# Expert outputs scattered by token, padding rows skipped, and the pair sum of the tail on PE

## The reference

```python
# 32 experts in 4 groups; each token takes the best group and its two best experts there
gate = softmax(top_v) * pg[group]
for each (token, k) with expert e:
    h = silu(x[token] @ w_gate[e]) * (x[token] @ w_up[e])     # 1024 -> 512
    y[token] += gate[token, k] * (h @ w_down[e])              # 512 -> 1024
x = layer_norm(alpha * x + y, ln3_g, ln3_b)
```

## Time and profile before

| | us |
|---|---|
| median of 3 runs | 1987.08 (1986.65 to 1987.32) |
| the profiled execution | 1967.48 |
| its span | 1965.7 |

### The profile page before, as it was taken

How to read it: one execution, slowest core, us unless ns; L and a number is a source line. 1 busy time by engine, 2 the same in 40 slices (tenths; PEclk the granted TensorE clock), 3 DMA queues, 4 the chain that set the end, 5 groups by cost and what they waited for, 6 DMA issues and landing times. The chain is left out here.

```text
span 1965.7 us, 33639 instructions
## 1 busy us (share of the span) xinstructions
PE 1787.5 (91%) x14867; PEld 1130.0 (57%) x14867; DVE 756.5 (38%) x1109; ACT 309.8 (16%) x705; POOL 209.9 (11%) x196
## 2 busy tenths in 40 slices
PE   8999999999999779999998999958999999999960
PEld 4455567776664554444666666525666666666630
DVE  1111456535362653430011433363343333333339
ACT  1111223311010441111000211000110111111115
POOL 2100000000000420000000000013111111111016
PEclk9999999999999769999999999968999999999985
DMA  5251002001100202134211000246999999999966
GB/s 199 89 176 43 1 1 88 1 1 43 43 1 0 93 8 110 43 123 139 83 43 43 22 22 22 92 189 241 422 424 423 424 424 424 424 424 424 423 239 218
DMA packets 72865, 326.96 MB, mean 166 GB/s; under 512 B 13369, under 2 KB 27969, under 8 KB 59729
## 3 DMA queue, kind: packets, MB, share of 16 engines
q1 hardware_dynamic: 47840, 280.70, 35.5%
q10 hardware_dynamic: 17360, 22.03, 3.5%
q0 software_dynamic: 7584, 23.08, 3.2%
HBM read 288.05 MB, written 37.65 MB: 166 GB/s over the span
## 5 line engine op out<-in xcount | busy, mean ns | idle before, releaser
L785 PE MATMUL psum<-arena 128*32 128x256 f32 x6144 | 339.3, 380 | 31.9 <-issue 30.7
L418 PE MATMUL psum<-arena 128*128 128x352 f32 x1152 | 342.4, 460 | 0.0
L427 PE MATMUL psum<-arena 128*128 128x512 f32 (+1 forms) x720 | 319.2, 602 | 5.1 <-DMA arena<-in_w_in 3.9
L785 PEld LDWEIGHTS psum<-arena 128*32 128x32 f32 x6144 | 232.0, 110 | 138.1 <-issue 45.1
L418 PEld LDWEIGHTS psum<-arena 128*128 128x128 f32 x1152 | 219.4, 191 | 122.4 <-issue 1.4
L1371 DVE COPY arena<-psum 128x512 f32<-128x512 f32 (+7 forms) x135 | 90.9, 681 | 418.1 <-PE psum L427 221.9
L427 PEld LDWEIGHTS psum<-arena 128*128 128x128 f32 (+1 forms) x720 | 132.0, 186 | 177.1 <-issue 175.2
L794 PE MATMUL psum<-arena 128*32 128x256 f32 x3072 | 172.4, 379 | 0.5 <-DVE arena L1776 0.5
L794 PEld LDWEIGHTS psum<-arena 128*32 128x32 f32 x3072 | 117.2, 110 | 49.3 <-DVE arena L1776 1.0
L1082 ACT ACTIVATE arena<-psum 128x128 f32<-128x128 f32 (+5 forms) x181 | 86.5, 495 | 349.8 <-PE psum L411 276.2
L1969 POOL DMA_INDIRECT arena<-x_rows,consts x102 | 96.7, 948 | 410.0 <-DVE arena L1779 381.8
(11 more groups left out here) (254 smaller groups left out, 1434.7 us busy)
## 6 DMA issues: line engine op xcount, KB each, us to landing
arena<-in_moe_w_down SPq DMA_DIRECT2D x34, 2048.0 KB, 15.6
arena<-in_moe_w_gate SPq DMA_DIRECT2D x34, 2048.0 KB, 14.9
arena<-in_moe_w_up SPq DMA_DIRECT2D x34, 2048.0 KB, 22.0
arena<-in_w_in SPq DMA_DIRECT2D x7, 2048.0 KB, 9.1
y_blocks<-arena ACTq DMA_DIRECT2D x136, 96.0 KB, 26.8
y_blocks<-arena ACTq DMA_DIRECT2D x1, 8448.0 KB, 43.9
arena<-in_x_prompt SPq DMA_DIRECT2D x9, 512.0 KB, 3.3
arena<-in_w_out SPq DMA_DIRECT2D x2, 2048.0 KB, 10.7
```

The costliest lines, as they stand in the source:

```text
L418: last = mm(ps[0:m, c * BANK:c * BANK + THIRD], lhs(k), rhs[:, k, c * THIRD:(c + 1) * THIRD], start=(k == 0), stop=(k == KD - 1))
L427: last = mm(ps[0:n, c * 512:(c + 1) * 512], lhs(k), rhs(k, c), start=(k == 0), stop=(k == KD - 1))
L785: last = mm(out, xeT[:, b, a, k, :], gu[b][:, :, k, j * P:(j + 1) * P], start=(k == 0), stop=(k == KD - 1))
```

## The change

- The DRAM tensor `y_blocks` gives way to `y_pairs` with 2 x 1056 + 1 rows: row 1 + 2 t + k belongs to token t and its k-th expert. Row 0 isn't used. `x2_rows` gets a row more as well, and token t stands in row 1 + t.
- The table made by PE now carries 1 + 2 t + k instead of t, so a padding row gives 0. From it DVE makes `tok_idx` (with a rounding that undoes the doubling, six operations instead of one before the cast) and `y_idx` (two operations). Padding rows get an index of 65536 and more, beyond the bound, and indirect DMAs skip such rows (`bounds_check`, `oob_is_err=False`).
- The results of a block are stored by POOL with three indirect DMAs (`scatter`), in place of ACT's four plain ones. POOL's order in the expert stage is gather(e), scatter(e-4), gather(e+1), ...
- In the tail SP loads `y_pairs` with plain DMAs, one for each tile, the tile of 32 tokens first (`TAIL`). PE adds the two rows of each token by two products with the identity into PSUM for the eight whole tiles; DVE does the small one. DVE's and ACT's steps are the same, in the order of `TAIL`.
- `dest_i`, `zeros`, the fill of the overflow blocks and the waits on it are gone. POOL in place of ACT sets `fin_ready`.

```diff
-            link(STT(TB_, EE, float(C), RR, ALU.mult, ALU.add))
-            link(V.tensor_copy(dest_i.rearrange("p k t -> p (k t)"), TB_))
...
-            link(TS(tokq, both[:, 0], 4.0, quarter, ALU.mult, ALU.add))
+            link(TS(tokq, both[:, 0], 0.5, -0.75, ALU.mult, ALU.add))
+            link(TS(tokq, tokq, ROUND, -ROUND, ALU.add, ALU.add))
+            link(TS(padq, both[:, 0], 0.0, FAR, ALU.is_equal, ALU.mult))
+            link(TS(padq, padq, quarter, None, ALU.add))
+            link(STT(tokq, tokq, 4.0, padq, ALU.mult, ALU.add))
+            link(TS(tokq, tokq, 4.0, None, ALU.add))
             V.tensor_copy(tok_idx, tokq).then_inc(tables_ready, 1)
+            dve.wait_ge(tables_ready, 1)
+            link(STT(tokq, both[:, 0], 4.0, padq, ALU.mult, ALU.add))
+            V.tensor_copy(y_idx, tokq).then_inc(tables_ready, 1)
```

```diff
 # SP
+            sp.dma_start(x2_dram[0:1, :], x2[0:1, 0, :]).then_inc(x2_stored, 16)
 # ACT, y_rows
                 last.then_inc(y_ready, 1)
-                act.wait_ge(y_ready, e + 1)
-                store_y(y_dram[bass.ds(e * C, C), :], slot, y_out[slot])
 # ACT, spilled
-                store_y(y_dram[bass.ds(j * C + NE * C, C), :], b, o_out)
-                act.wait_ge(o_out, 64 * j + 64)
```

```diff
 # POOL
+            def scatter(e, slot, done):
+                for a in range(NS):
+                    pool.indirect_dma_start(out=y_quarters, in_=ye[slot][:, a, :], in_offset=None,
+                                            out_offset=bass.IndirectOffsetOnAxis(ap=y_idx[:, e, a:a + 1], axis=0),
+                                            bounds_check=4 * (2 * T + 1) - 1, oob_is_err=False)\
+                        .then_inc(done, 16)
+            for e in range(2, NE):
+                pool.wait_ge(xt_ready, e - 1)
                 gather(e, e % 2, xe_in[e % 2])
+                if e >= 4:
+                    scatter_expert(e - 4)
...
+                    pool.wait_ge(o_y, j + 1)
+                    scatter(NE + j, j % 2, o_out)
+                    pool.wait_ge(o_out, 48 * j + 48)
+                    link(Q.memset(quarter, 0.0))
+            for i in range(4):
+                pool.wait_ge(y_out[i], 48 * NE // 4)
+            Q.memset(quarter, 0.0).then_inc(fin_ready, 1)
```

```diff
 # SP
+            sp.wait_ge(fin_ready, 1)
+            for t in TAIL:
+                rows = y_dram[1 + 2 * t * P:1 + 2 * (t * P + rows_of(t)), :]
+                sp.dma_start(pairs[0:rows_of(t), t], rows.rearrange("(t k) n -> t k n", k=2)).then_inc(g_in[t], 16)
 # PE
+            for u in range(1, NT):
+                t = TAIL[u]
+                pe.wait_ge(g_in[t], 16)
+                if u >= 5:
+                    pe.wait_ge(sum_ready, u - 3)
+                for c in range(2):
+                    for k in range(2):
+                        last = mm(PAIR[u % 4][:, c * 512:(c + 1) * 512], ident, pairs[:, t, k, c * 512:(c + 1) * 512],
+                                  start=(k == 0), stop=(k == 1))
+                last.then_inc(pair_ready, 1)
```

More of the change, by code:

```diff
@@ L97, in build @@
         quarter = const(1)
-        dest_i = const(2 * NT).bitcast(U32).rearrange("p (k t) -> p k t", t=NT)
+        y_idx = const(NB * NS).bitcast(U32).rearrange("p (n a) -> p n a", a=NS)
         over_f = const(NOVER + 1)
@@ L400, in build @@
         HG = [(h, c) for h in range(HH) for c in range(NT)]
+        PAIR = [psum[:, 2 * i * BANK:2 * i * BANK + D] for i in range(4)]
         block = ctx.enter_context(nc.Block())
@@ L1276, in _ @@
                          for a in (0, 2)]
[L1278 to L1281, removed]
             def y_rows(e, b, slot, turn_n):
@@ L1346, in _ @@
                             spilled(2 * i + b, b)
-            for i in range(4):
-                act.wait_ge(y_out[i], 64 * NE // 4)
-            A(rstd[:, 1:2], eps_ln, ACT.Copy).then_inc(fin_ready, 1)
-            for t in range(NT):
+            for u, t in enumerate(TAIL):
                 n = rows_of(t)
@@ L1945, in _ @@
             Q.iota(e_rev, [[-1, NE]], base=NE, channel_multiplier=0, allow_small_or_imprecise_dtypes=True)
-            Q.iota(tokf, [[P, NT]], base=0, channel_multiplier=1, allow_small_or_imprecise_dtypes=True)
+            for k in range(2):
+                Q.iota(tokf[:, k, :], [[2 * P, NT]], base=k + 1, channel_multiplier=2, allow_small_or_imprecise_dtypes=True)
             Q.iota(blk_iota, [[1, NB]], base=0, channel_multiplier=0, allow_small_or_imprecise_dtypes=True)
@@ L1979, in _, with scatter_expert @@
+            def scatter_expert(e):
+                pool.wait_ge(y_ready, e + 1)
+                scatter(e, e % 4, y_out[e % 4])
+            gather(0, 0, xe_in[0])
+            gather(1, 1, xe_in[1])
+            for i, n in enumerate(("ln3_g", "ln3_b")):
+                pool.dma_start(ln3_par[:, i, :], io[n].to_broadcast([P, D])).then_inc(ln3_loaded, 16)
+            pool.wait_ge(tables_ready, 2)
+            for e in range(2, NE):
+                pool.wait_ge(xt_ready, e - 1)
                 gather(e, e % 2, xe_in[e % 2])
+                if e >= 4:
+                    scatter_expert(e - 4)
@@ L1980, in _ @@
             n_over = pool.value_load(over_i[0:1, NOVER:NOVER + 1], min_val=0, max_val=NOVER)
+            scatter_expert(NE - 4)
+            with pool.If(n_over > 0):
+                pool.wait_ge(xt_ready, NE - 1)
+                gather(NE, 0, o_x[0])
+            scatter_expert(NE - 3)
+            with pool.If(n_over > 1):
+                pool.wait_ge(xt_ready, NE)
+                gather(NE + 1, 1, o_x[1])
+            scatter_expert(NE - 2)
+            scatter_expert(NE - 1)
             for j in range(NOVER):
@@ L1995, in _ @@
[L1995 to L2005 removed]
+                        gather(NE + j, j % 2, o_x[j % 2])
```

121 lines of the change are left out of this document (45 added, 76 removed).

## The result

| | before | after |
|---|---|---|
| median of the runs, us | 1987.20 (1986.65 to 1988.98) | 2083.82 (2077.99 to 2086.60) |
| ratio after / before, 95% interval | | 1.048 (1.046 to 1.050) |
| span of the profiled execution, us | 1965.7 | 2084.8 |
| start of the first L785, us | 1339.96 | 1344.71 |
| from there to the last expert's L785, us | 506.2 | 618.9 |

The forecast was 1959.8 us, faster by 27; the kernel is slower by 97. The last four rows cut both spans in the same places: +4.7, +112.7, +8.7, -7.0. So the loss lies in the expert stage, and the tail gave a gain. The two profiles lie 119 us apart and the timed medians 97, because the profiled execution of the kernel before was some 20 us quicker than its timed ones.

What follows compares the result with a forecast made beforehand. The prediction took the expert stage to be bound by DMA time (queues 101.3%), after a PE-bound opening. Start +1.9, experts -16.0, spilled blocks -1.4 and tail -11.8 gave -27.3: 1987.1 to 1959.8 us, range 1949 to 1977.

Steps and rivals of the forecast that it cites:

- Cost nothing: Expert stage: moving the stores from ACT's to POOL's queue, six issues taking 7.5 of 16 us a step, costs no time.
- the cover of gather(e + 1): Expert stage: this gather, issued some 3.7 us later behind the scatter, still lands before L779's successor-free need, over one step away.
- Rival (d): Expert stage: POOL becomes the bound if an issue takes above 2.59 us; at 2.7, 2015 us in all; chance 4%.
- Experts, DMA time: Expert stage: skipped rows save 0.55 us of DMA time per expert, 29 experts, -16.0 us; DMA-bound step 16.1 us.
- The opening at 15.54 us: First expert steps, bound by PE: should last about twice as many experts as before.
- Start: Before the first gather: five more DVE operations for the token table, +1.9 us.
- Spilled blocks: Two blocks after the experts: without ACT's store issues PE no longer waits in the first, -1.4 us.
- Tail: From the last scaled y rows (Y) to the end: 52.4 us instead of 64.2, -11.8 us; loads start at Y + 6.9.
- rival (c): Tail: PE stays at 1.2 GHz because its work comes in pieces, +11.9 instead of -11.8, 1983.5 us; chance 7%.
- (a): Expert stage: skipped rows keep their full DMA price, experts gain 0, 1975.8 us; chance 14%.
- (b): Expert stage: the saving is larger and PE becomes the bound, -27 instead of -16, 1948.8 us; chance 10%.
- The base: Whole kernel: differences taken from the profile are added to the timed median, 1987.1 us, 19.6 above the profiled execution.

Runs made afterwards that it cites:

- before_again: The kernel before, unchanged, profiled in another execution; 1980.88 us, ratio 1.000.
- ticked: The changed kernel with POOL's six indirect DMAs of an expert step spread, waiting for thirds of PE's products; 1957.66 us, 0.989 of the kernel before.
- ticked_fin: ticked with POOL's twenty empty branches for spilled blocks that do not occur put under one more branch; 1955.85 us, 0.989 of the kernel before.
- ticked_full: ticked without the skip: places without a token fetch row 0 and store to spare rows; 1972.76 us, 0.992 of the kernel before.
- ticked_head: ticked_fin with the twelve gathers of the first four experts spread as well; 1956.93 us, 0.988 of the kernel before.
- before_ticked: The kernel before with only its gathers spread as in ticked_head, stores still on ACT's queue, no skip; 1973.79 us, ratio 0.995.
- before_bounds: The kernel before with the bounds check added to its gathers, no index out of bounds; 1974.10 us, ratio 0.996.

## Why the prediction was wrong

**The step that failed** is the one that ended "Cost nothing": the stores moved to POOL's queue. The sum of issue times, 7.5 of 16 us, was right (7.6), as was the cover of gather(e + 1), which nobody had to wait for. What it didn't ask is what six issues without a pause do to another engine. It looked for a victim in POOL's queue and behind POOL's semaphores, and PE is in neither. In its steps the kernel before had never more than three in a row, and the profile that the prediction was built on was of an execution in which not even the six at the head made PE pause (see before_again), so it held no hint. Price: 112.7 us between the first and the last expert's L785, where -16.0 stood.

**Rival (d)** had the side and the place right and the mechanism wrong. An issue took 0.98 to 1.08 us (the very first gather 1.27), far from the 2.59 at which POOL would bound the stage. The Trainium skill's rule that stood beside it (SBUF — State Buffer, "SBUF: two separate sides") would have made POOL's issues slow; here they stayed fast, and PE stood still. (The page's 3.1 us are those of a whole DMA, not of its issue.) No run shows that rule at work in this stage.

**Experts, DMA time.** Right in kind, a little too large. Without the rows of issues (ticked) the step is 16.09 us, where I had 16.1 for a DMA-bound one, and from expert 1 to expert 31 it took 480.4 us against 494.4 in the first profile of before: -14.0 for -16.0. The opening at 15.54 us lasted six steps (seven in ticked_fin) against five, not twice as many. Two things shared the gain: 0.42 a step from the skip, for which I had 0.55, and 0.15 from the stores' move (16.66 to 16.51 in ticked_full, where gathers and stores take 1.96 us of DMA time for 1.00 + 1.10 before), for which I had nothing. So that the step came out at 16.1 is in part luck.

**Start.** Five more operations: L1748 at 1334.24 to the first gather at 1337.43, 3.19 us against 1.55 before, from L1756 at 1331.17 to its first gather at 1332.72: +1.6 for +1.9. The other 3.1 of the 4.7 were there when L1748 began; where they come from is open. PE starts its first L785 between 1339.0 and 1341.5 us in the four profiles with the old table and no work added on POOL, and between 1341.9 and 1344.7 in the eight with the new one.

**Spilled blocks.** -1.4 forecast, +8.7 measured. The last expert's own gate and up falls into this stretch, beside the last row of six, and most of the loss is there: it takes 16.3 us to the first L794, where the kernel before took 10.6. Behind it ACT's store issues are gone, but POOL's come in rows of three, and PE pauses in L794 and L840:

```profile
1971.68 0.62 PE L785 MATMUL psum<-arena 128*32 128x256 f32 x4 [0.82 <-issue]
...
1994.72 0.98 POOL L1981 DMA_INDIRECT y_pairs<-arena,consts  x1 [3.38 <-ACT arena L1293]
...
1997.30 0.98 POOL L1981 DMA_INDIRECT y_pairs<-arena,consts  x1 [0.30 <-issue]
1999.04 6.03 PE L840 MATMUL psum<-arena 128*32 128x256 f32 x106 [0.34 <-issue]
1999.21 0.28 ACT L1325 ACTIVATE arena<-psum 128x128 f32<-128x128 f32 x1 [5.26 <-remote]
```

L1325 of the first spilled block comes late for another reason than before. ticked_fin, which has no row of six there but left the rows of three as they are, still had 59.2 us against 55.3.

**Tail.** -7.0 for -11.8. Rows of after, with Y = 2027.57:

```profile
2028.35 0.98 POOL L1981 DMA_INDIRECT y_pairs<-arena,consts  x1 [11.76 <-ACT arena L1336]
...
2033.08 0.10 POOL L2019 MEMSET consts<- 128x1 f32 x1 [1.17 <-DMA y_pairs<-arena,consts]
2037.83 0.10 POOL L2022 MEMSET consts<- 128x1 f32 x1 [4.65 <-issue]
2037.95 4.31 SPq L1076 DMA_DIRECT2D arena<-y_pairs  x9
...
2050.02 1.22 DVE L1859 SCALAR_TENSOR_TENSOR arena<-arena,psum 128x1024 f32<-128x1024 f32 x1 [6.31 <-PE psum L874]
...
2074.60 1.20 DVE L1859 SCALAR_TENSOR_TENSOR arena<-arena,psum 128x1024 f32<-128x1024 f32 x1
```

The loads start at Y + 10.4, not Y + 6.9: between the two memsets POOL spends 4.65 us, which I had at nothing. Some 1.6 to 2.7 of them are the branches of blocks that aren't there (ticked_fin), the rest is open. From tile 0's landing (Y + 15.85) to its sum read by DVE it takes 6.6 us, not 5.2, because PE's first pair products run at 1.2 GHz for longer: the granted clock is back at 1.00 at 2049.2 us, 5.8 behind the first L874 at 2043.42, where I had taken 3.1 from the earlier trace rows. 3.5 + 1.4 is the missing 4.8. The rest held: 24.6 us from the first L1859 of a whole tile to the last (24.7 forecast), 10.2 from there to the end (10.2), no DVE operation over 1.3 us, and the clock back at 1.00 while the pairs run (columns as in the earlier trace rows), so rival (c) falls:

```profile
2041.30:2048.00 6.70, 4.58 (x6) 1.98 (x7) 2.38 (x2) 3.08 (x7) 0.00 (x0) 0.50 1.01 419
2048.00:2051.00 3.00, 3.00 (x7) 1.28 (x6) 0.98 (x1) 0.00 (x0) 0.00 (x0) 0.80 1.00 423
2051.00:2074.00 23.00, 23.00 (x54) 9.88 (x52) 21.97 (x20) 20.17 (x46) 0.00 (x0) 1.00 0.63 263
```

**The other rivals.** (a) falls with ticked_full, (b) with ticked's 16.09.

**The base.** The differences were taken from a profile and added to the median of timed runs 19.6 us above it. The better part of that gap is likely the pauses of the kind that the change made larger (12.9 of the 14.2 us between the two profiles of the kernel before); no trace of the executions of that first comparison shows it. That ticked's 1957.7 us lies 2 us from the 1959.8 forecast is therefore partly chance: by its medians the change without rows of issues is worth 16.9 us against its like (ticked_head against before_ticked), not 27, and the other part of ticked's gain is that it freed the old gathers of their pauses.

## What to carry to other kernels

Before work moves to POOL's queue, count how many indirect DMAs it will then issue without a pause, not only their sum: here two in a row cost nothing, three about 1 us, four about 2, six 4.2 to 5.2 us of PE's time. Where a row would form, let each issue wait for a point of PE's progress that passes anyway, or put POOL's other work between them. And a gap between the timed median and the profiled execution can mean that the profile is of an execution unlike the others: here a second profile of the unchanged kernel showed pauses that the first had not at all. A pause is dear only where its engine bounds the stage: the same 1.1 us cost 0.16 us a step where PE would have waited for DMA.

## What the hardware showed that I had not expected

- A row of indirect issues on POOL holds up PE, both its products and its weight loads, with no wait in either queue. It begins 2.8 to 3.1 us after the first of the row and ends about a microsecond behind the last. Within it PE gets some 6 products in 0.76 us at first, then 4 or 5 in 1.44 us.
- The price goes by the issues and how close they stand (1.25 to 1.31 us): in the mean of the experts 0.9 to 1.1 us behind three and 4.2 to 5.2 behind six, and 1.8 to 2.5 us in the eleven rows of four that six of the traces have (one is step 19 of after). It doesn't go by bytes (1 KB or 256 B a place), descriptors (768 or 480 a step), direction, bounds check, or skipped rows. Plain DMAs of POOL (128 x 256 bytes) and its arithmetic (1.5 us) between them do nothing of the kind. What the two engines share there isn't settled: no view shows it, and that it is PE's supply of instructions is argued from the idle time marked issue alone. The DMA queue that brings instructions in packets of 16 KB (q8) isn't it: between 1434 and 1964 us of after it moves none, and the pauses go on.
- Executions of one kernel differ in this. The first profile of before has no pause behind its rows of three nor behind the six at its head; the second has 1.08 us a step and more at its head. The five profiles with a row of six in each step all have the pauses, and before_bounds and before_again have them beside the six at the head too, 3.7 and 3.5 us.
- After a pause of some 4 us PE may go on at 1.2 GHz for 3.4 us: eight of 28 steps, 1.3 us each.
- A skipped row is nearly free: with 34% of the rows skipped POOL's queue took 1.34 in place of 1.96 us an expert, 32% less. But only two thirds of what it saved reached the step.
- POOL passing twenty branches that aren't taken took some 1.6 to 2.7 us.
